# Two small VectorE jobs of an attention loop given to GpSimd: the gate factor and the low part of finished rows

## The reference, cut to what matters

```
p_sel = masked_softmax(s_sel, m_sel)
o_sel = einsum('bqghk,bgqkd->bqghd', p_sel, v_sel)
...
g = sigmoid(gate_logits).reshape(B, S, 3, N_KV, HPG)[..., None]
o = g[:, :, 0] * o_cmp + g[:, :, 1] * o_sel + g[:, :, 2] * o_w
return o.reshape(B, S, ATTN_W)
```

## Time and profile before

| what | value |
|---|---|
| time, median of 3 runs | 3253.02 us (3251.45 to 3257.33) |
| the profiled execution's own time | 3255.08 us |
| its span in the trace | 3253.3 us |
| TensorE matmul busy | 3137.6 us (96%) |
| VectorE busy | 1969.9 us (61%) |
| ScalarE busy | 1097.2 us (34%) |
| GpSimd busy | 1667.4 us (51%) |
| chain that ended last | PE 86%, DVE 9%, ACT 2%, issue 2%, DMA 1%, POOL 0% |

### The profile page before, as it was taken

How to read it: one execution, slowest core, us unless ns; L and a number is a source line. 1 busy time by engine, 2 the same in 40 slices (tenths; PEclk the granted TensorE clock), 3 DMA queues, 4 the chain that set the end, 5 groups by cost and what they waited for, 6 DMA issues and landing times.

```text
span 3253.3 us, 40834 instructions
## 1 busy us (share of the span) xinstructions
PE 3137.6 (96%) x15045; PEld 2562.7 (79%) x15045; DVE 1969.9 (61%) x2607; ACT 1097.2 (34%) x1985; POOL 1667.4 (51%) x1781
## 2 busy tenths in 40 slices
PE   8999999998899999999999999989979999999998
PEld 6888887676788888888878788867758888888887
DVE  7883256887546666555578732678865545555555
ACT  2124414666212222222220243256751222222233
POOL 3547632233454656666745385322334556666665
PEclk8999999999999999999999999999989999999999
DMA  7454541000522222111234546200005211111112
GB/s 253 148 194 133 159 125 27 1 1 1 201 65 73 71 78 78 52 52 52 78 130 139 191 143 185 73 4 1 1 28 193 59 52 52 52 52 52 52 46 104
DMA packets 299053, 280.98 MB, mean 86 GB/s; under 512 B 10859, under 2 KB 275303, under 8 KB 298344
## 3 DMA queue, kind: packets, MB, share of 16 engines
q1 hardware_dynamic: 279410, 207.66, 21.9%
q10 hardware_dynamic: 19446, 70.72, 5.9%
HBM read 232.20 MB, written 38.80 MB: 83 GB/s over the span
## 4 chain that ended last, share of the span: by engine, by line
PE 86%; DVE 9%; ACT 2%; issue 2%; DMA 1%; POOL 0%; ACTq 0%; DVEq 0%; POOLq 0%
PE lin L1328 47%; PE lin L1727 16%; PE lin L1475 8%; PE aux L1618 2%; DVE pTL L2492 2%; PE pv L1634 2%; PE pv L1635 1%; DVE negm L2468 1%; PE lin L1594 1%; PE lin L1595 1%; PE pv L1433 1%; ACT pTH L2049 1%; PE lin L1560 1%; DVE adared L630 1%; PE lin L1378 1%
## 5 line engine op out<-in xcount | busy, mean ns | idle before, releaser
L1297 POOL TENSOR_SCALAR unit<-wraw 128x512 fp32r<-128x512 f32 x340 | 285.1, 839 | 785.2 <-PE lin L1328 327.2
L1328 PE MATMUL lin<-hH,unit 128*128 128x512 f32 x1824 | 576.7, 392 | 3.5 <-POOL wlo L1299 3.5
L1328 PE MATMUL lin<-hL,unit 128*128 128x512 f32 x1824 | 572.6, 389 | 0.0
L1328 PE MATMUL lin<-hH,wlo 128*128 128x512 f32 x1824 | 572.4, 389 | 0.0
L1299 POOL TENSOR_TENSOR wlo<-wraw,unit 128x512 fp32r<-128x512 f32 x340 | 485.2, 1427 | 28.3
L1727 PE MATMUL lin<-fH,unit 128*128 128x512 f32 x1568 | 486.7, 390 | 4.8 <-DVE xT L2628 4.8
L2628 DVE SCALAR_TENSOR_TENSOR xT<-lin,adac,xT 128x512 f32<-128x512 f32 x448 | 328.8, 748 | 182.6 <-PE lin L1727 177.8
L1176 POOL TENSOR_SCALAR prob<-prob,fac 128x640 f32<-128x640 f32 (+7 forms) x256 | 183.5, 717 | 445.0 <-DVE fac L2462 427.1
L1328 PEld LDWEIGHTS lin<-hH,wlo 128*128 128x128 f32 x1824 | 342.4, 188 | 72.0
L1328 PEld LDWEIGHTS lin<-hL,unit 128*128 128x128 f32 x1824 | 342.4, 188 | 71.6 <-issue 0.2
L1328 PEld LDWEIGHTS lin<-hH,unit 128*128 128x128 f32 x1824 | 339.6, 188 | 73.8 <-issue 5.3
(11 more groups left out here) (333 smaller groups left out, 5588.7 us busy)
## 6 DMA issues: line engine op xcount, KB each, us to landing
wraw<-in_w_ff SPq DMA_DIRECT2D x136, 512.0 KB, 4.0
wraw<-in_w_ada SPq DMA_DIRECT2D x80, 512.0 KB, 4.5
wraw<-in_w_in SPq DMA_DIRECT2D x72, 512.0 KB, 4.4
mix_keep<-tmp ACTq DMA_DIRECT2D x32, 512.0 KB, 6.1
wraw<-in_w_o SPq DMA_DIRECT2D x24, 512.0 KB, 4.0
adar<-in_w_ada SPq DMA_DIRECT2D x16, 512.0 KB, 11.8
x_keep<-xT ACTq DMA_DIRECT2D x4, 2048.0 KB, 9.3
gate_keep<-ropes ACTq DMA_DIRECT2D x16, 512.0 KB, 3.6
```

The costliest lines, as they stand in the source:

```text
L1297: pool.tensor_scalar(high, raw, 1.0, 1.0, ALU.mult, ALU.mult).then_inc(w_hi, 1)
L1328: mm = pe.matmul(lin[c % 2][:, hf], w, m(k, hf), start=first, stop=last)
```

## The change

GpSimd's scaling takes two factors per row from memory, the reciprocal and the gate, where it had one and the constant 1.0. VectorE's `factors` makes the reciprocal alone and signals behind it. The subtraction that makes atL goes from VectorE's step fin + 3 to GpSimd's step fin + 3, behind that step's scalings, with the same wait for `o_hi`; it signals `fin_lo` as before.

```diff
--- before.py
+++ after.py
@@ -1172,9 +1172,17 @@
                             for i in range(HPG):
                                 if st["last"] + SCALED_AFTER[i] == u:
                                     pool.wait_ge(f_made, set0 + st["no"] + 1)
-                                    p = prob_of(st["no"], i)[:, 0:st["n"]]
-                                    pool.tensor_scalar(p, p, fac[:, st["no"] % 2, i:i + 1], 1.0, ALU.mult, ALU.mult).then_inc(p_scaled, 1)
+                                    p, gt = prob_of(st["no"], i)[:, 0:st["n"]], BRANCH[st["b"]] * NH + HPG * st["g"] + i
+                                    pool.tensor_scalar(p, p, fac[:, st["no"] % 2, i:i + 1], gates[:, st["qt"], gt:gt + 1],
+                                                       ALU.mult, ALU.mult).then_inc(p_scaled, 1)
                                     pool.wait_ge(p_scaled, HPG * (set0 + st["no"]) + i + 1)
+                        for st in SETS:
+                            if st["b"] == "s" and st["fin"] + 3 == u:
+                                k = NKV * NTH[st["qt"]] + st["g"]
+                                pool.wait_ge(o_hi, k + 1)
+                                at_ = (slice(None), slice(2 * st["g"], 2 * st["g"] + 2), slice(st["qt"] * P, (st["qt"] + 1) * P))
+                                pool.tensor_tensor(atL[at_], att.rearrange("p (j t) -> p j t", j=2), atH[at_].bitcast(F32),
+                                                   ALU.subtract).then_inc(fin_lo, 1)
 
                 def pair_forms(n):
 
@@ -2457,9 +2465,7 @@
                     dve.wait_ge(exp_made, m + HPG)
                     if no >= 2:
                         dve.wait_ge(p_scaled, HPG * (set0 + no - 1))
-                    then(dve.reciprocal(f, sums[:, m:m + HPG]))
-                    gt = BRANCH[st["b"]] * NH + HPG * st["g"]
-                    dve.tensor_tensor(f, f, gates[:, st["qt"], gt:gt + HPG], ALU.mult).then_inc(f_made, 1)
+                    dve.reciprocal(f, sums[:, m:m + HPG]).then_inc(f_made, 1)
 
                 def maximum(u):
                     dve.wait_ge(s_done, u + 2)
@@ -2511,11 +2517,6 @@
                                 pick = lambda t: t.rearrange("p (j o t) -> p j o t", j=2, o=2)[:, :, odd, :]
                                 dve.tensor_tensor(att[HD * odd:HD * (odd + 1), :].rearrange("p (j t) -> p j t", j=2),
                                                   pick(pv[0:HD, st["g"], :]), pick(low_half), ALU.add).then_inc(fin_sum, 1)
-                        if st["fin"] + 3 == u:
-                            dve.wait_ge(o_hi, k + 1)
-                            at_ = (slice(None), slice(2 * st["g"], 2 * st["g"] + 2), slice(st["qt"] * P, (st["qt"] + 1) * P))
-                            dve.tensor_tensor(atL[at_], att.rearrange("p (j t) -> p j t", j=2), atH[at_].bitcast(F32),
-                                              ALU.subtract).then_inc(fin_lo, 1)
 
 
                 for i in range(KC + 1):
```

## The result

The changed kernel took 3260.13 us (median of 11 runs, 3256.63 to 3263.35), the kernel before 3253.78 us (11 runs, 3251.27 to 3257.33). The ratio is 1.0020, with a 95% interval of 1.0012 to 1.0027: 6.35 us slower, just inside 0.2% and within the range given, 2 us more than the forecast of +4.4. The interval, 3.9 to 8.8 us, holds the forecast too, so these 2 us are not clear of noise.

The account below looks back on a forecast made before the run. TensorE was read as fullest, VectorE second, with few of the removed instructions on the chain. Per layer 0.8 + 2.5 + 0.2 + 0.8 − 2.1 = +2.2 us, both layers +4.4, gave 3257.4 us, range 3250 to 3264.

Parts of the forecast that it names:

- The end of attention: Each layer's end: last transposes 0.8 us late, projection 2.5 us later behind GpSimd's last low part and queued weight split.
- The last transposes: Set 31, last of a layer: 0.20 us earlier, then 0.82 later by set 29's low part and 0.20 by second factors.
- set 27: Transposes of set 27 in attention: 0.98 us spare, said to just hold, so no loss counted.
- Set 23: Transposes of set 23 in attention: 0.39 us spare, so 0.43 late, half of it, 0.2 us a layer, reaching the end.
- The start of the projection: Projection after attention: TensorE starts at half clock, and the length of this stretch was kept unchanged.
- The second factor: GpSimd's scalings: a second factor from memory costs 0.05 us each, 0.2 us for a set's four.
- Rival 2: GpSimd's scalings: the second factor is dear, deciding from about 0.12 us; at 0.2 us, 3262.7 us; chance 0.16.
- The collision: Sets 6 and 10: VectorE's two-input lines wait for GpSimd, 0.4 us each, 0.8 us a layer, bounds 0 and 1.5.
- The gain: VectorE's removed multiplications and atL subtractions in attention: 2.1 us a layer gained, bounds 1.0 and 2.9.
- the split behind the last low part: Sign of being right: GpSimd's line 1297 for ("ua", 0) starts behind the last atL.
- VectorE as the pace of everything: Attention: VectorE sets the pace, so all removed time comes back, 3233 us; chance 0.06 with other ways over 0.2% faster.
- A free end: End of attention: split not queued behind the last low part, or projection has slack; 2 × 2.5 falls away, 3252.4 us; chance 0.06.

Follow-up runs that it names:

- e2: Only the low part (atL) moved to GpSimd, factors still made by VectorE, against the kernel before: 3260.79 us, ratio 1.0021.
- e3: Changed kernel with only the last low part of each layer (set 31) back on VectorE: 3253.92 us, ratio 1.0001 to the kernel before.
- e8: Changed kernel with GpSimd splitting the projection's first tile ahead of the last low part: 3254.22 us, ratio 1.0004 to the kernel before.
- e1: Only the two-factor scaling, atL staying on VectorE, against the kernel before: 3253.42 us, ratio 1.0000.
- e5: e3 with the low part moved behind the fourth scaling only in sets 4, 6, 8 and 10: 3251.69 us, ratio 0.9995 to the kernel before.
- e11: e4 with GpSimd also waiting for the last low part before splitting the projection's second tile: 3249.41 us, ratio 0.9991 to the kernel before.
- e10: e4 repeated unchanged: 3249.57 us, ratio 0.9994 to the kernel before.
- e4: e3 with every low part that fell between a set's scalings moved behind the fourth scaling: 3246.73 us, ratio 0.9980 to the kernel before.

## Why the prediction was right, and where not

**The end of attention** was the heart of the forecast and held. The wait behind the last atH grew by 2.36 us where 2.5 stood. e2, e3 and e8 show that it is this one instruction, and that 2.05 of it is the work queued behind it. The last transposes came 0.65 us later where 0.8 stood. The low part lengthened GpSimd's row by 0.7 us rather than 0.82. The four scalings took 0.14 longer rather than 0.20, though the second factor was dearer than forecast: before, one of them had taken 0.54 instead of 0.38, beside VectorE's own low part.

**What was wrong: set 27.** "Sets 19 and 27 have 0.86 and 0.98 spare and just hold" is true of 19 only (0.29 us spare now). The 0.98 of set 27 was read where TensorE ran at half clock (0.50 granted, 813 to 814) and so reached the transposes late. At full clock in the changed kernel it waits 1.05 and 1.07 us for GpSimd there, and the chain goes through set 27's low part and scalings in both layers. In e1, without the low part, the transposes of layer 0 start 3.01 us behind the reciprocal instead of 3.69: up to 0.7 us a layer that the sum had at nothing. **Set 23** came as forecast: its transposes start 4.13 us behind the reciprocal's start (785.18 to 789.31), before 3.59 (784.46 to 788.05), 0.54 later; 0.43 stood.

**The start of the projection** may have been mis-sized too: "I keep this stretch as long as it is". Its half clock lasted 5.0 us instead of 3.4 in layer 0, and the last mxH is made 49.5 and 49.9 us behind the projection's start, before 48.7 and 48.7. But this differs between executions without any such wait. With c at 1.5 us or less, 24 starts in twelve traces had 2.9 to 6.1 us at half clock (mean 3.7); the four starts of e2 and the changed kernel, with c at 2.95, had 4.1 to 6.0 (mean 5.1). By the means that is 1.3 us more at half clock, about 0.7 us of work a layer, a tendency and not more.

**The second factor** costs 0.072 us, not 0.05. The forecast took 0.10 for the first factor from the mean of the earlier trace rows, 0.724, which mixes in scalings that were held up; from the median, 0.696, the first costs 0.076. Rival 2 has not happened: it needed 0.12.

**The collision** is there. Lines 2420 and 2423 together take 1.62 us before and 2.12 after in set 6, 1.52 and 2.03 in set 10, in both layers: 2.0 us in all, where the sum had 1.6. e5 takes it away with the low parts. e11 shows the mechanism on one instruction, 0.42 us alone against 1.15 us beside GpSimd. The Trainium skill ("SBUF — State Buffer", "Who interferes with whom") says that a VectorE instruction with two SBUF inputs contends with a GpSimd instruction that reads SBUF; that agrees with these rows. VectorE's line 2498, whose one input lies in PSUM, took 0.67 us at 618.50 beside a running scaling, and never more than 0.70 in that trace.

**The gain** of 2.1 us a layer is the weakest term. Column a of the changed kernel is 4.0 and 1.8 us shorter than before, but with 10 and 3 us less half clock, one trace each. By the estimate it is 1.1 longer in layer 0 and as long in layer 1, where the forecast comes to 1.1 shorter (0.2 + 0.8 − 2.1). e2 says the same: the factor half showed no gain in this placement. It showed one only once the low parts stood behind the scalings.

**So how good was it?** The place and the size of the main loss were right. That the total came within 2 us is in part luck, as the gain was not there to be seen and measured times differ by 3 us between groups. Of the signs, the split behind the last low part, TensorE's wait for GpSimd and line 2431 at 1.12 came as said; VectorE is 16.8 us less busy in the whole kernel (1969.9 to 1953.1), not 24, as its waits in collisions count as busy.

**The rivals.** VectorE as the pace of everything (3233 us) is out: TensorE's wait for VectorE's low parts fell by 1.6 us, not by 5. A free end (3252) is what e3 and e8 had to build first, and they measure 3254.

## What to carry to other kernels

An instruction that is moved to an emptier engine takes with it everything that stands behind it in that engine's program: look for the last instance of a loop, where the next stage's preparation is queued, and leave that one where it was, or put the preparation first. Inside the loop, place the moved work behind what another engine waits for, not in front of it. With these two moves the change turned from 6.4 us slower into about 4.5 us faster. And before calling a place safe for its spare time, look at the clock: a spare that is read where TensorE runs at half clock is gone when it runs at full clock.

## What the runs showed of the hardware

VectorE's subtraction with two SBUF inputs (128x256) takes 0.42 us alone and 1.15 us when it starts 0.39 us into a GpSimd subtraction of 1.27 us; it ends 0.27 us behind it. It goes the other way too: GpSimd's scaling of 128x640 takes 1.24 us instead of 0.88 when VectorE's line with two SBUF inputs gets ahead of it.

On GpSimd a factor read from memory, one per row, adds 0.072 to 0.076 us to a scaling: 0.62 with none (line 1297), 0.696 with one and 0.768 with two, medians at 128x512.

How long TensorE runs at half clock in the attention differs between executions of one and the same kernel (e10: 4.3 and 3.4 us in a; e4, the same kernel: 0.4 and 4.2). That this is also why two medians of one kernel differ by 3 us is likely, but not shown: there is no trace of every run.
